# Two token tiles requested from another queue, and 25 small operations moved behind the token scales, in a hybrid decoder step

## The reference, cut to what matters

```python
def rmsnorm(x, g):
    return x * lax.rsqrt(jnp.mean(x * x, axis=-1, keepdims=True) + RMS_EPS) * g
...
xn = rmsnorm(x, g_pre)
u, gate = jnp.split(xn @ w_in, 2, axis=-1)          # x: 1032 rows of 2048
...
log_a = -LRU_C * r * jax.nn.softplus(-lam)          # lam: the decay parameter, 2048 values
```

## Time and profile before

| | us |
|---|---|
| median of 3 runs (lowest to highest) | 2923.12 (2919.98 to 2924.32) |
| the profiled execution | 2920.77 |
| its span, first to last instruction | 2918.7 |
| TensorE matmul busy in the span | 2788.2 (96%) |
| VectorE busy | 1235.0 (42%) |
| ScalarE busy | 800.8 (27%) |

### The profile page before, as it was taken

The page is one execution under the profiler, slowest core; times in us unless marked ns, Lnnn a source line. Parts: engine busy times, 40 slices in busy tenths (PEclk is TensorE's granted clock), DMA queues, the critical chain, the costliest instruction groups (busy, mean ns, idle before and its releaser), DMA issues.

```text
span 2918.7 us, 51373 instructions
## 1 busy us (share of the span) xinstructions
PE 2788.2 (96%) x17620; PEld 2692.0 (92%) x17620; DVE 1235.0 (42%) x2900; ACT 800.8 (27%) x1856; POOL 1408.6 (48%) x2117
## 2 busy tenths in 40 slices
PE   5999999999996999899999999999999999899997
PEld 5999999999996999898899989998899889899996
DVE  8444354344436001563745175406541654400234
ACT  4123113302314002542422042204320332200343
POOL 1344354345434555566455645564456454455552
PEclk8999999999998999999999999999999999899997
DMA  8321112111123334872111211111111113333676
GB/s 269 103 62 51 54 58 66 43 63 61 53 65 140 97 98 153 271 244 81 38 49 58 61 41 48 59 59 36 55 57 60 37 44 106 118 95 97 191 247 210
DMA packets 386505, 277.30 MB, mean 95 GB/s; under 512 B 16248, under 2 KB 363705, under 8 KB 385209
## 3 DMA queue, kind: packets, MB, share of 16 engines
q1 hardware_dynamic: 310602, 187.84, 21.3%
q10 hardware_dynamic: 75720, 87.18, 8.9%
HBM read 217.19 MB, written 62.10 MB: 96 GB/s over the span
## 4 chain that ended last, share of the span: by engine, by line
PE 87%; DVE 7%; DMA 2%; issue 2%; ACT 1%; POOL 0%; SPq 0%; DVEq 0%; ACTq 0%; POOLq 0%
PE ps L537 53%; PE ps L618 22%; PE ps L576 3%; PE ps L683 2%; PE ps L709 2%; PE ps L696 2%; DVE xsp L1250 1%; DMA raw<-in_a_w_out 1%; DVE xsp L1314 1%; DVE xsp L1662 1%; DVE xsp L1246 1%; DVE gb L1288 1%; DMA out_y_prompt<-stg 0%; ACT pt L1081 0%; DVE q L1545 0%
## 5 line engine op out<-in xcount | busy, mean ns | idle before, releaser
L537 PE MATMUL ps<-xsp,wsp 128*128 128x344 f32 (+2 forms) x10080 | 1642.4, 321 | 3.8 <-issue 3.8
L537 PEld LDWEIGHTS ps<-xsp,wsp 128*128 128x128 f32 x10080 | 1586.0, 188 | 43.8 <-issue 41.7
L618 PE MATMUL ps<-xsp,wsp 128*128 128x320 f32 (+1 forms) x4608 | 745.0, 324 | 42.3 <-DVE xsp L1314 9.4
L618 PEld LDWEIGHTS ps<-xsp,wsp 128*128 128x128 f32 x4608 | 736.5, 191 | 46.2 <-issue 11.1
L419 POOL CAST wsp<-raw 128x512 fp32r<-128x512 f32 x272 | 216.6, 796 | 722.5 <-PE ps L537 366.6
L424 POOL TENSOR_SCALAR raw<-raw,prm 128x128 f32<-128x128 f32 x640 | 234.3, 384 | 495.2 <-PE ps L537 467.2
L421 POOL TENSOR_TENSOR wsp<-raw,wsp 128x512 fp32r<-128x512 f32 x272 | 401.9, 1478 | 50.5 <-POOL wsp L419 50.5
L1410 DVE TENSOR_TENSOR acc<-acc,stg 128x640 f32<-128x640 f32 (+1 forms) x64 | 71.0, 1109 | 561.3 <-ACT stg L964 326.9
L457 POOL TENSOR_TENSOR wsp<-raw,wsp 128x512 fp32r<-128x512 f32 x128 | 172.7, 1362 | 139.8 <-ACT wsp L938 139.7
L431 POOL TENSOR_TENSOR wsp<-raw,wsp 128x512 fp32r<-128x512 f32 x160 | 209.8, 1311 | 29.3 <-POOL wsp L428 29.3
L428 POOL TENSOR_SCALAR wsp<-raw 128x128 fp32r<-128x128 f32 x640 | 175.4, 301 | 31.2 <-POOL raw L424 31.2
(11 more groups left out here) (201 smaller groups left out, 2367.9 us busy)
## 6 DMA issues: line engine op xcount, KB each, us to landing
raw<-in_a_w_in SPq DMA_DIRECT2D x128, 256.0 KB, 2.8
raw<-in_a_w_out SPq DMA_DIRECT2D x128, 256.0 KB, 2.8
raw<-in_b_w_qg SPq DMA_DIRECT2D x128, 256.0 KB, 2.8
raw<-in_b_w_out SPq DMA_DIRECT2D x128, 256.0 KB, 2.7
o_t<-stg ACTq DMA_DIRECT2D x32, 320.0 KB, 2.2
xsp<-o_t ACTq DMA_DIRECT2D x8, 1280.0 KB, 7.0
xsp<-x_t ACTq DMA_DIRECT2D x8, 1280.0 KB, 11.2
xr<-in_x_prompt SPq DMA_DIRECT2D x8, 1024.0 KB, 8.0
```

The lines of the kernel that those rows point to most:

```text
L537: return pe.matmul(ps[:, b0 + g, 0:w], wsp[:, slots[j], wh, k, :], xsp[:, kk, xh, at:at + w], start=(j == 0 and k == 0 and n == 0), stop=( ...
L618: op = pe.matmul(ps[:, b0 + g, 0:w], wsp[:, j, wh, k, :], xsp[:, j * QK + k, xh, at:at + w], start=(j == 0 and k == 0 and n == 0), stop=(j ...
```

## The change

The loop on SyncE that requests the token tiles starts at tile 2. Tiles 0 and 1 are requested by ScalarE, before its first wait. On VectorE the 25 operations from `hbr` to `nsp4` move from ahead of the first tile's split to behind the nine diagonals; the code between keeps its order. The two operations on lam (L1223, L1224) stay, and so does ScalarE's exponential.

```diff
-        for n in range(9):
+        for n in range(2, 9):
             slot = n % 3
...
         act.sem_inc(S["fin_sb"], 2)
+        for n in range(2):
+            act.dma_start(xr[:, n, :], t["x_prompt"][0, n * P:(n + 1) * P, :]).then_inc(S[f"x_in{n}"], 16)
         act.wait_ge(S["x_turned"], 1)
...
         dve.tensor_tensor(spt[:, 0, :], lam, spt[:, 2, :], ALU.max).then_inc(S["root_in"], 1)
+        for n in range(9):
+            w = P if n < 8 else NB
+            cols = slice(n * P, n * P + w)
+            dve.wait_ge(S["x_staged"], (n + 1) * NQ)
...
+            if n >= 2:
+                dve.wait_ge(S["diag_mm"], n - 1)
+            dve.tensor_scalar(dg[0:w, n % 2, 0:w], ident[0:w, 0:w], sxs[0:w, 1, n:n + 1], None, ALU.mult).then_inc(S["diag"], 1)
         own.step(dve.tensor_scalar(hbr[:], prm[:, :, R_BR], 0.5, None, ALU.mult))
         own.step(dve.tensor_scalar(hbi[:], prm[:, :, R_BI], 0.5, None, ALU.mult))
         own.link(dve.tensor_scalar(spt[:, 2, :], spt[:, 2, :], 0.0, 2.0, ALU.max, ALU.mult))
...
         own.step(dve.tensor_scalar(nsp4[:], sp2[:], -2.0, None, ALU.mult))
-        for n in range(9):
-            w = P if n < 8 else NB
-            cols = slice(n * P, n * P + w)
...
-            dve.tensor_scalar(dg[0:w, n % 2, 0:w], ident[0:w, 0:w], sxs[0:w, 1, n:n + 1], None, ALU.mult).then_inc(S["diag"], 1)
         dve.wait_ge(S["diag_mm"], 9)
         dve.wait_ge(S["bias_out"], 16)
         own.step(dve.tensor_copy(rstd[:, 0:512], ps[:, 6, :]))
```

More of the change, by code:

```diff
@@ L1224, in _ @@
         dve.tensor_tensor(spt[:, 0, :], lam, spt[:, 2, :], ALU.max).then_inc(S["root_in"], 1)
[L1225 to L1240, removed]
         for n in range(9):
@@ L1270, in _ @@
             dve.tensor_scalar(dg[0:w, n % 2, 0:w], ident[0:w, 0:w], sxs[0:w, 1, n:n + 1], None, ALU.mult).then_inc(S["diag"], 1)
+        own.step(dve.tensor_scalar(hbr[:], prm[:, :, R_BR], 0.5, None, ALU.mult))
+        own.step(dve.tensor_scalar(hbi[:], prm[:, :, R_BI], 0.5, None, ALU.mult))
+        own.link(dve.tensor_scalar(spt[:, 2, :], spt[:, 2, :], 0.0, 2.0, ALU.max, ALU.mult))
+        dve.wait_ge(S["root_done"], 1)
+        e_, s_, s2_ = spt[:, 1, :], spt[:, 0, :], spt[:, 3, :]
+        own.link(dve.tensor_scalar(s_, e_, 2.0, None, ALU.add))
+        own.link(dve.reciprocal(s_, s_))
+        own.link(dve.tensor_tensor(s_, s_, e_, ALU.mult))
+        own.link(dve.tensor_tensor(s2_, s_, s_, ALU.mult))
+        own.link(dve.tensor_scalar(sp2[:], s2_, 1.0 / 17.0, 1.0 / 15.0, ALU.mult, ALU.add))
+        for n in (13, 11, 9, 7, 5, 3, 1):
+            own.link(dve.tensor_tensor(sp2[:], sp2[:], s2_, ALU.mult))
+            own.link(dve.tensor_scalar(sp2[:], sp2[:], 1.0 / n, None, ALU.add))
+        own.link(dve.scalar_tensor_tensor(out=sp2[:], in0=sp2[:], scalar=4.0, in1=s_, op0=ALU.mult, op1=ALU.mult))
+        own.link(dve.tensor_tensor(sp2[:], sp2[:], spt[:, 2, :], ALU.add))
+        own.step(dve.tensor_scalar(nsp4[:], sp2[:], -2.0, None, ALU.mult))
         dve.wait_ge(S["diag_mm"], 9)
```

## The result

The changed kernel takes 2928.18 us (median of 20 runs, 2923.03 to 2932.97) against 2922.2 us (20 runs) before: a ratio of 1.0019, 95% interval 1.0013 to 1.0026. It is 6.0 us slower; no change was forecast, with 2926.5 as the upper end. The profiled execution reads 2931.48 us with a span of 2929.7.

The account below looks back on a forecast made before the run. TensorE was taken to set the end (87% of the span), VectorE the opening. Terms: -3.23 tile landing, +3.2 tables and parameters, 0 issue slots, 0 for the 25 operations; sum 0.0, forecast 2923.1 us, range 2918.5 to 2926.5.

Parts of the forecast that it names:

- The requests leave early, the tile stops being the limit: Opening: ScalarE issues tiles 0 and 1 at 1.89, so tile 0's landing no longer holds the first copy; -3.23 us.
- The collision is on the engine of the single rows: Opening: tile packets join the one DMA engine carrying the 8 KB parameter rows, delaying parameters and tables; +3.2 us.
- P: Time the parameters have landed and their turning starts: 9.08 before, forecast 10.5 to 12.5; first copy possible at P + 3.95.
- each lets one tile packet pass: Queues alternate packets on that engine: 11 remaining parameter packets each let one tile packet by, 3.4 us at most.
- The tables decide: Opening: the tables, landing after the parameters, set the first copy at 14.6 to 17.95 against 16.26; -1.6 to +1.7 us.
- T: Time the table loads are complete: 11.96 before, forecast 13.6 to 16.9; first copy possible at T + 1.04.
- the rival with the loss: Opening: tables come last, waiting for all 16 tile packets with no pause filled; +1.7, up to +3 us, chance 0.18.
- The 25 operations are hidden: Before the second `evac`: 4.6 us of delay fit VectorE's 5.83 us idle time, 1.2 remain; cost 0.
- A start later by d moves the end by d: From VectorE's first split: starting it d earlier or later moves everything behind by d, if later tiles keep pace.

Follow-up runs that it names:

- e4: The changed kernel, but ScalarE waits for the parameters to have landed before it issues the two tile requests; ratio 1.0012 to the kernel before.
- e7: The changed kernel, but SyncE requests tiles 0 and 1, only after the parameters are turned and copied; ratio 1.0009 to the kernel before.
- e10: The changed kernel, but ScalarE requests tiles 0 and 1 only after the parameters are turned and copied; ratio 1.0025 to the kernel before.
- e12: The changed kernel, but SyncE requests tiles 0 and 1, only after ScalarE's exponential for the decay parameter; ratio 1.0008 to the kernel before.
- e6: The changed kernel, but ScalarE requests only tile 0 early and tile 1 stays on SyncE; ratio 1.0012 to the kernel before.
- e2: The kernel before with only the 25 operations moved, the tiles still requested by SyncE; ratio 1.0002 to the kernel before.
- in-line kernels: Versions of the changed kernel with tiles 0 and 1 on SyncE behind the parameters, ahead of the tables, table work after the first split; ratios 0.9987 to 1.0003.
- e1: The kernel before with only the two tile requests moved to ScalarE, the 25 operations left in place; ratio 1.0028 to the kernel before.
- e3: The changed kernel with each single parameter row written as 16 pieces, though the rows travelled as before; ratio 1.0020 to the kernel before.
- e5: The changed kernel with tiles 0 and 1 on SyncE behind the parameters, tables last, VectorE's table work after the first split; ratio 0.9988 to the kernel before.
- e9: As e5, but with the 25 operations back ahead of the first split; ratio 0.9995 to the kernel before.
- e11: As e5, plus two spare 1 MB copies requested on ScalarE's queue near 125 us; ratio 0.9994 to the kernel before.
- e13: As e5, but with tile 2 requested by ScalarE; ratio 1.0001 to the kernel before.
- e18: As e5, plus two small spare copies of two 8 KB rows each on ScalarE's queue near 125 us; ratio 0.9995 to the kernel before.

## Why the prediction was wrong

- **The requests leave early, the tile stops being the limit:** right. Tile 0 waits for the parameters' copies.
- **The collision is on the engine of the single rows:** right in kind. The last packets of the opening are 8 KB packets at about 6% of 16 engines. Taking the tiles out of the way (e4, e7, e10, e12) brings P back, and halving them (e6) brings back about half.
- **"each lets one tile packet pass", P up by 1.4 to 3.4:** this step failed. P went up by 6.24. From 4 to 7 us ScalarE's queue moved 165 packets with 1.23 MB, on average some nine rows of 8 KB on each engine, and SyncE's one small packet. The bound let 11 of an engine's 16 tile packets pass; in fact the last rows waited for all 16, which is 16 x 0.31 = 4.95. Of the other 1.3, 0.3 is slower issue; packets that were slower beside the tables, as the one of 0.86 us, can be the rest, but no run parts it. The step took the equal counts of the earlier trace rows, two queues late in a steady stream, for the rule of a start. It gives the late start of 3.33 us; by that alone the time would have been 2922.2 + 3.3 = 2925.5, inside the range of the prediction. The rest is the last point's.

The Trainium skill (DMA: Bandwidth & Descriptors, Queues, rings and completion order) says more than the prediction took from it: an engine that turns between queues drains a whole packet, typically 9 to 17 descriptors, from one before it turns to the next. If one 8 KB row of the profile is one such descriptor, a tile puts 8 on each engine, and a tile passes as a block. The rows from 4 to 7 us agree with that; those from 12 to 14, with one or two tile packets to a row, do not. No run here explains the difference.

- **The tables decide:** wrong, though T = 16.50 is inside its 13.6 to 16.9. The parameters, later than their bound, came last: P + 3.98 = 19.30, against T + 1.04 = 17.54 for the tables. So the rival with the loss (+1.7 to +3, chance 0.18) had the right sign and came near the 3.04 of the first copy, but by luck: it charged the tables, and the parameters cost it. For the whole, 6.0, its price was half.
- **The 25 operations are hidden:** right. e2 says 1.0002; of VectorE's 5.83 us idle time 1.98 are left in the changed kernel (1.2 forecast).
- **A start later by d moves the end by d:** right up to TensorE's take-over (3.33 at the split, 3.33 at 82.72), not shown behind it. From there 6.0 - 3.3 = 2.7 us of the median's loss are not accounted for; the prediction had nothing for them, and they carry the time out of its range. The interval of the ratio reaches from 3.8 to 7.6 us, and the start, read from one profile, can itself be off by more than a microsecond (the spread of P in the in-line kernels); e1 and e3 start 3.8 and 3.7 late and lose 8.2 and 5.8. In the profiled execution the clock took 2.3 us (1.22 in the first chunk, 1.08 in the 270 matmuls); in e1 and e3, which start later still, the two took 9.59 and 42.59, and 9.58 and 42.59, so a late start as such does not cost that. ScalarE's tile requests go together with the excess in all eight kernels that have them, but the tests that were meant to single them out did not, and the cause stays open.

## What to carry to other kernels

In this opening, bulk data that was requested early on a second queue did not fill gaps: it went ahead of the small loads that everything waits for, and these paid for each of its packets. Put the small loads first and the bulk behind them in one queue, and let what is not needed at once (tables, derived constants) follow; that order gained about 3 us where the second queue lost 6. When two queues must share, look for rows of the same stretch of the program before taking turns for granted, and put the price of all of the other queue's packets into the upper bound.

## What was unexpected of the hardware

- Two queues that moved 48 and 49 packets in 1 us later on the earlier trace rows moved 0 or 1 and 47 to 68 at the start (4 to 7 us).
- A tile packet of 8 KB held its engine for 0.86 us instead of 0.31 while SyncE's queue moved 181 small packets (11 to 12 us of the changed kernel).
- A contiguous row of 8 KB, written as 16 x 128, moved in the same number of packets as before (746 on SyncE's queue); written as pieces with gaps, it made SyncE's later issues come 9.1 us later.
- The same parameters, on the same queue with the same neighbours, were ready between 8.48 and 11.13 us after the start in the nine profiles of the in-line opening (e5, e9, e11, e13 to e18).
